# An expert loop in groups of four, with one token gather per group: a mixture-of-experts stage on one core

## The chip, the cores and the metric

One Trainium2 chip, one core of it. The metric is device time in microseconds (us) of one execution; less is better. All arithmetic is fp32 or fp32r (the form of fp32 that the kernel uses for products of a high and a low part).

## The reference, cut to what matters

A two-layer backbone over 256 latent tokens of width 1024 (with 256 context tokens in layer 0). Layer 0 has attention, a pooling mixer and a dense SwiGLU; layer 1 has a Fourier mixer and a top-2-of-8 expert SwiGLU. Only the last is touched:

```
logits = h @ router_w                      # (256, 8)
top_v, top_i = top_k(logits, 2); top_p = softmax(top_v)
gates  = sum(one_hot(top_i, 8) * top_p)    # (256, 8), two entries per token
y = 0
for e in range(8):
    y = y + gates[:, e:e+1] * ((silu(h @ w1[e]) * (h @ w3[e])) @ w2[e])   # widths 1024 -> 3584 -> 1024
```

h is 256 tokens x 1024, the weights of one expert are 42 MB (42 pieces of 1 MB), and they are all read from HBM once. The final RMSNorm follows.

## The kernel before, in words

**Routing.** After the Fourier mixer, TensorE computes the logits, turns them to token rows, turns h to token rows (h_tok, four banks copied by ScalarE, line 793) and, while VectorE ranks the tokens of each expert, runs a few matmuls on constants to fill the time (keep_warm). VectorE writes a table of ranks (line 1172), then the first choice of slots (picks(0), line 1200), then the gate values and the number of turns that the loops make (gates(), line 1176), in that order in its program.

**One turn** handles one expert and 96 of its tokens (CAP = 96). Two rounds would be made if an expert had more than 96 tokens; the trace shows eight turns, so one round. In a turn:

- gather (line 1625, TensorE): for every block of 128 rows of h, matmuls of h_tok with a 0/1 matrix pick (tokens x slots) put the 96 chosen tokens into banks 5 and 6. These are fp32 matmuls with 32 stationary columns each, four of them side by side in the array: 64 matmuls with 96 moving columns, which the trace records as 128. ScalarE (line 800) and VectorE (line 1211) copy the two banks to x_e, the x of this expert.
- up (line 1649) for four phases of the 3584 hidden units: w1 and w3 against x_e, 32 slots as the stationary operand, in banks 0 to 2. Line 1661 is its matmul.
- ScalarE takes silu (line 817), VectorE multiplies (line 1240) and turns blocks of 32 (line 1244).
- down (line 1666) for four phases, in banks 3 and 4. Line 1674 is its matmul.
- y of an expert is taken in the next turn (lines 807 and 1218), and TensorE spreads it back to its tokens with fp32r matmuls (combine, line 1636, matmul at 1641), which VectorE adds to x (line 1226).
- spreads (line 1681, matmuls at 1685 and 1689) makes the turned matrices for that.

**The order of the work** is written out by hand in each engine's program; semaphores join them. TensorE's turn i (expert, line 1692) is up and down of phases 0 to 3 with the rest of the previous expert between them; near its end it gathers for turn i + 1 (line 1723), and the last down of the turn covers the copies of that gather. Turn 0 is written out once in front (line 1728), and turns 1 to 7 are the body of a loop whose number of turns is read from memory (line 1732); ScalarE and VectorE have the same form (lines 836 and 1269). Ninth and last is a gather for a turn that is never made.

**The weights** are sent by SyncE's queue (line 500) into a ring of 16 slots of 1 MB, step by step: 12 steps a turn, and the pieces of a step are sent when TensorE has finished the step four before. This part has its own loop and isn't changed.

Of the kernel before, what the change touches and what calls it, by code (L numbers as in the profile page):

```python
# [15 lines left out]
P = 128  # L16
# [21 lines left out]
QUAD = 32  # L38
TRIPLES = CAP // QUAD
MAX_ROUNDS = -(-T // CAP)  # L40
TABLE = EXPERTS * (MAX_ROUNDS + 1)

# [134 lines left out]
def build(nc, vec_d, con_d, rope_d, x_d, ctx_d, ada_d, mixa_d, mixb_d, attn_d, mixout_d, ffn_d,  # L177
          dft_d, fnet_d, router_d, moe_d, out_d):
    ctx = ExitStack()
    with ctx:  # L180
# [10 lines left out]


        split = nc.alloc_sbuf_tensor_at("split", [P, 7 * PIECE], F32R, offset=ring_at + 4 * RING)
        xT = sb("xT", KD * T)
# [61 lines left out]
        ada_sum = view(work, 0, 2, 512)  # L256
        h_tok = view(work, 0, 2, D)
        x_e = view(work, 2048, KD, CAP)
        pick = view(work, 2816, 2, 2, P)
        rank_at = view(work, 3328, 2, TABLE)  # L260
# [18 lines left out]
        y_parts = [view(split, 4 * PIECE + n * D, D) for n in range(2)]  # L279
        spread = view(split, 4 * PIECE + 2 * D, 2, T)  # L280

        def plain(ap):
# [44 lines left out]
            sem("gap_ready"), sem("odds_ready"), sem("mask_ready"), sem("rank_ready"), sem("loops_ready"))  # L327
        pick_ready, gathered, x_first, x_second = sem("pick_ready"), sem("gathered"), sem("x_first"), sem("x_second")
        e_used, e_gate, e_hidden, e_turned = sem("e_used"), sem("e_gate"), sem("e_hidden"), sem("e_turned")
        y_high, y_low = ([sem(f"{name}{n}") for n in range(2)] for name in ("y_high", "y_low"))  # L330
# [277 lines left out]
        def _(act):  # L608
# [182 lines left out]
            for f in range(4):  # L791
                act.wait_ge(tok_ready, f + 1)
                nc.scalar.activation(h_tok[:, f // 2, (f % 2) * 512:(f % 2) * 512 + 512], bank[f][:, :], ACT.Copy).then_inc(tok_taken, 1)
# [24 lines left out]

            def expert(i):
                first = isinstance(i, int)  # L820
# [9 lines left out]
                take_gathered(i + 1)  # L830

            take_gathered(0)
            expert(0)
            act.wait_ge(loops_ready, 1)
            turns = act.value_load(loops[0:1, 0:1], min_val=EXPERTS, max_val=EXPERTS * MAX_ROUNDS)
            with nc.Fori(1, turns, engines=bass.OrderedEngineSet([act.engine]), hint_back_edge=True) as i:
                expert(i)
            take_y(turns, 0)

# [6 lines left out]
        def _(dve):  # L846
# [329 lines left out]
            def gates():  # L1176
# [15 lines left out]
                link(nc.vector.tensor_reduce(cols(210, 1), more, AX_X, ALU.add))  # L1192
                link(nc.vector.tensor_scalar(cols(211, 1), cols(210, 1), float(EXPERTS), float(EXPERTS), ALU.mult, ALU.add))
                link(nc.vector.tensor_scalar(cols(212, 1), cols(210, 1), 1.0, None, ALU.add))
# [12 lines left out]

            def take_gathered(i):

                dve.wait_ge(gathered, i + 1)  # L1210
                nc.vector.tensor_copy(x_e[:, 4:8, :], bank[6][:, 0:4 * CAP].rearrange("p (a b) -> p a b", a=4)).then_inc(x_second, 1)

# [32 lines left out]

            def expert(i):
                first = isinstance(i, int)
# [12 lines left out]
                hidden(i, 2)  # L1260
                hidden(i, 3)
                take_gathered(i + 1)

            picks(0)
            gates()
            take_gathered(0)
            expert(0)
            turns = dve.value_load(loops[0:1, 0:1], min_val=EXPERTS, max_val=EXPERTS * MAX_ROUNDS)
            with nc.Fori(1, turns, engines=bass.OrderedEngineSet([dve.engine]), hint_back_edge=True) as i:
                expert(i)  # L1270
            take_y(turns)
# [12 lines left out]
        def _(pe):  # L1284
# [363 lines left out]

            def up(i, phase, half, first):

# [5 lines left out]
                for k in range(4):  # L1656
                    for g in range(TRIPLES):
                        if half == 0 and k == 0 and not (first and phase == 0):
                            pe.wait_ge(e_hidden, PHASES * TRIPLES * i + TRIPLES * (phase - 1) + g + 1)
                        for c in range(4):  # L1660
                            last = mm(bank[g][c * QUAD:(c + 1) * QUAD, 0:count * P],  # L1661
                                      x_e[:, 4 * half + k, g * QUAD:(g + 1) * QUAD], source[:, :, k, :, c, :],
                                      start=(half == 0 and k == 0), stop=(half == 1 and k == 3), skip_group_check=True)
# [17 lines left out]
            def spreads(i):  # L1681

                for n in range(2):
# [7 lines left out]

            def expert(i):
                first = isinstance(i, int)
                pe.wait_ge(x_first, i + 1)
                pe.wait_ge(x_second, i + 1)
                up(i, 0, 0, first)
                up(i, 0, 1, first)
                if not first:
                    down(3, PHASES * TRIPLES * i, i, STEP_LAST)
                up(i, 1, 0, first)  # L1700
                if not first:
                    pe.wait_ge(spread_taken, i)
                    for pair in range(3):
                        combine(i, pair)
                up(i, 1, 1, first)
                if not first:
# [7 lines left out]
                spreads(i)  # L1714
                up(i, 2, 0, first)
                up(i, 2, 1, first)
                down(1, PHASES * TRIPLES * i + 6, i, STEP_OF["down", 1])
                up(i, 3, 0, first)
                up(i, 3, 1, first)
# [11 lines left out]
            turns = pe.value_load(loops[0:1, 0:1], min_val=EXPERTS, max_val=EXPERTS * MAX_ROUNDS)  # L1731
            with nc.Fori(1, turns, engines=bass.OrderedEngineSet([pe.engine]), hint_back_edge=True) as i:
                expert(i)
            down(3, PHASES * TRIPLES * turns, turns, 0)
            pe.wait_ge(x_first, turns + 1)
            pe.wait_ge(x_second, turns + 1)
            for pair in range(3):
# [72 lines left out]
```

## Time and profile before

| what | value |
|---|---|
| time, median of 3 runs | 1423.32 us (1421.16 to 1425.7) |
| the profiled execution | 1426.97 us |
| its span (first to last instruction) | 1425.2 us |
| mean granted TensorE clock | 0.991 of full |
| TensorE busy | 96% of the span |
| VectorE, ScalarE, GpSimd busy | 29%, 17%, 2% |
| HBM read | 454.76 MB, 320 GB/s over the span |
| expert turns, from the first up to the last down | 472.08 to 1409.74 us |

The page gives busy shares and the chain that ended last; the chain can also be asked for in order of time, and there each piece has its start, its length and what it was. A piece called issue is time in which the engine waited for nothing that the profile shows. L1661 is line 1661 of the kernel before.

### The profile page before, as it was taken

How to read it: one execution, taken by the hardware profiler on the slowest of the kernel's cores; microseconds unless marked ns; L12 is line 12 of the kernel's file. 1: busy time of each engine (PE TensorE's matmuls, PEld its weight loads, DVE VectorE, ACT ScalarE, POOL GpSimd, SP SyncE). 2: the span in 40 equal slices, each digit the busy share in tenths (PEclk: the TensorE clock that was granted, in tenths of full speed). 3: DMA queues.
4: the chain of work that ended last, by engine and by line, in shares of the span. 5: the costliest groups of instructions: out<-in, count | busy, mean ns of one | idle time of the engine just before them, and what ended most of it. 6: DMA issues, size and time to landing. Idle time of an engine off the chain costs nothing.

```text
span 1425.2 us, 30939 instructions
## 1 busy us (share of the span) xinstructions
PE 1364.1 (96%) x13838; PEld 737.1 (52%) x13838; DVE 412.2 (29%) x778; ACT 243.4 (17%) x410; POOL 21.7 (2%) x36
## 2 busy tenths in 40 slices
PE   5899899999999999999999999999999999999997
PEld 3755799999968434433433433423343353343334
DVE  2555579888434200010011001101001101110102
ACT  2444543333434100000000000000000000000002
POOL 2300000000000000000000000000000000000000
PEclk9899999999999999999999999999999999999999
DMA  9666259996616597997997999899799799889960
GB/s 382 258 237 237 94 222 354 353 372 259 226 41 275 219 364 305 418 418 299 396 414 295 415 389 374 337 383 422 288 417 418 295 414 410 358 351 410 422 277 31
DMA packets 58783, 457.83 MB, mean 321 GB/s; under 512 B 6656, under 2 KB 6784, under 8 KB 7584
## 3 DMA queue, kind: packets, MB, share of 16 engines
q1 hardware_dynamic: 58656, 455.84, 79.6%
q8 instruction: 116, 1.90, 0.5%
q14 instruction: 11, 0.09, 0.0%
HBM read 454.76 MB, written 1.05 MB: 320 GB/s over the span
## 4 chain that ended last, share of the span: by engine, by line
PE 94%; DVE 2%; issue 2%; DMA 1%; ACT 1%; SPq 0%; DVEq 0%; PEldq 0%; ACTq 0%
PE bank L1661 41%; PE bank L1674 20%; PE bank L1552 9%; PE bank L1542 4%; PE bank L1369 3%; PE bank L1632 2%; PE bank L1300 1%; PE bank L1406 1%; PE bank L1641 1%; PE bank L1473 1%; PE bank L1341 1%; PE bank L1576 1%; PE bank L1480 1%; PE bank L1588 1%; PE bank L1329 1%
## 5 line engine op out<-in xcount | busy, mean ns | idle before, releaser
L1661 PE MATMUL bank<-ring,work 128*32 128x512 f32 (+1 forms) x6144 | 588.6, 542 | 13.6 <-issue 11.9
L1661 PEld LDWEIGHTS bank<-ring,work 128*32 128x32 f32 x6144 | 208.4, 110 | 382.0 <-issue 348.3
L1674 PE MATMUL bank<-ring,moe 128*32 128x512 f32 x2688 | 294.9, 592 | 0.0
L1240 DVE TENSOR_TENSOR moe<-moe,bank 128x256 f32<-128x256 f32 (+1 forms) x96 | 31.5, 383 | 648.7 <-ACT moe L817 648.7
L1674 PEld LDWEIGHTS bank<-ring,moe 128*32 128x32 f32 x2688 | 99.1, 110 | 180.7 <-issue 179.2
L817 ACT ACTIVATE moe<-bank 128x256 f32<-128x256 f32 (+1 forms) x96 | 27.4, 358 | 737.0 <-PE bank L1661 737.0
L1552 PE MATMUL bank<-split 128*128 128x256 f32 x1056 | 131.2, 284 | 0.7 <-PE bank L1329 0.6
L1552 PEld LDWEIGHTS bank<-split 128*128 128x128 f32 x1056 | 128.0, 192 | 2.1 <-ACT split L748 1.3
L913 DVE TENSOR_TENSOR split<-ring,split 128x2048 fp32r<-128x2048 f32 x33 | 75.6, 2291 | 31.3 <-ACT split L754 24.3
L754 ACT ACTIVATE split<-ring 128x2048 fp32r<-128x2048 f32 x32 | 61.3, 1914 | 114.7 <-PE bank L1552 86.0
L928 DVE SCALAR_TENSOR_TENSOR work<-ring,condp,work 128x512 f32<-128x512 f32 x84 | 63.2, 752 | 3.7 <-DVE split L913 0.9
L1542 PE MATMUL bank<-split 128*128 128x256 f32 x480 | 59.5, 283 | 0.3 <-PE bank L1329 0.3
L1542 PEld LDWEIGHTS bank<-split 128*128 128x128 f32 x480 | 58.2, 192 | 0.4 <-issue 0.4
L1369 PE MATMUL bank<-split 128*128 128x256 f32 x384 | 47.0, 284 | 3.6 <-DVE split L1069 1.8
L1369 PEld LDWEIGHTS bank<-split 128*128 128x128 f32 x384 | 46.3, 192 | 4.1 <-DVE split L1069 2.2
L1226 DVE SCALAR_TENSOR_TENSOR xT<-bank,ada,xT 128x256 f32<-128x256 f32 x64 | 26.3, 472 | 62.2 <-PE bank L1641 62.2
L1406 PE MATMUL bank<-split 128*128 128x256 f32 (+1 forms) x192 | 31.5, 329 | 4.5 <-ACT split L624 4.0
L862 DVE TENSOR_TENSOR split<-ring,split 128x1024 fp32r<-128x1024 f32 (+1 forms) x24 | 28.5, 1207 | 15.9 <-ACT split L624 15.5
L1406 PEld LDWEIGHTS bank<-split 128*128 128x128 f32 x192 | 28.0, 205 | 7.8 <-ACT split L624 4.4
L1244 DVE STREAM_TRANSPOSE moe<-moe 128x256 f32<-128x256 f32 (+1 forms) x96 | 31.7, 381 | 0.0
L1204 DVE TENSOR_SCALAR work<-con,work 128x128 f32<-128x128 f32 x36 | 7.9, 282 | 75.1 <-PE bank L1689 75.1
L1300 PE MATMUL bank<-ring,condp 128*32 128x128 f32 x768 | 25.1, 286 | 4.5 <-DMA ring<-in_ada 4.0
(195 smaller groups left out, 730.4 us busy)
## 6 DMA issues: line engine op xcount, KB each, us to landing
ring<-in_moe SPq DMA_DIRECT2D x336, 1024.0 KB, 10.6
ring<-in_ffn SPq DMA_DIRECT2D x16, 2048.0 KB, 8.4
ring<-in_ada SPq DMA_DIRECT2D x12, 2048.0 KB, 8.8
ring<-in_ada SPq DMA_DIRECT2D x24, 1024.0 KB, 7.0
ring<-in_mixout SPq DMA_DIRECT2D x2, 2048.0 KB, 9.4
ring<-in_fnet SPq DMA_DIRECT2D x2, 2048.0 KB, 9.4
ring<-in_mixa SPq DMA_DIRECT2D x1, 2048.0 KB, 11.6
ring<-in_mixb SPq DMA_DIRECT2D x1, 1664.0 KB, 13.3
```

The source lines that it names most:

```text
L754: nc.scalar.activation(high_d[:, q % SPLITS_DENSE, :], piece_view(q), ACT.Copy).then_inc(high_ready, 1)
L913: nc.vector.tensor_tensor(low_d[:, q % SPLITS_DENSE, :], piece_view(q), plain(high_d[:, q % SPLITS_DENSE, :]), ALU.subtract).then_inc(low_ ...
L928: ins = nc.vector.scalar_tensor_tensor(out=total, in0=half_view(h)[:, k, :], scalar=weight, in1=total, op0=ALU.mult, op1=ALU.add)
L1240: nc.vector.tensor_tensor(gate_e[:, g, 0:n], gate_e[:, g, 0:n], bank[g][:, n:2 * n], ALU.mult).then_inc(e_hidden, 1)
L1244: nc.vector.transpose(hiddenT[phase % 2][:, g, 0:n], gate_e[:, g, 0:n]).then_inc(e_turned, 1)
L1300: last = mm(bank[RUNS[run][2]][32 * j:32 * j + 32, u * P:(u + 1) * P], cond[:, k, :], w[:, k, j * P:(j + 1) * P], start=(k == 0), stop=(k ...
L1369: last = mm(bank[banks[c // 2]][:, (c % 2) * T:(c % 2) * T + T], parts[left][:, k, j * P:(j + 1) * P], source[right][:, k0 + k, :], start= ...
L1406: last = mm(out, parts[left][:, k, lo:hi], h_in[right][:, k0 + k, 0:n], start=((left, right) == PRODUCTS[0] and k0 + k == 0 and opens), st ...
L1542: last = mm(bank[FFN_BANKS[k // 2]][:, (k % 2) * T:(k % 2) * T + T], w[:, j, k * P:(k + 1) * P], hidden_parts[g % 2][:, right, j, :], star ...
L1552: last = mm(bank[kind == "w3"][:, j * T:(j + 1) * T], w[:, k, j * P:(j + 1) * P], h_parts[:, right, k, :], start=(n == 0 and j == 0 and k ...
L1661: last = mm(bank[g][c * QUAD:(c + 1) * QUAD, 0:count * P], x_e[:, 4 * half + k, g * QUAD:(g + 1) * QUAD], source[:, :, k, :, c, :], start= ...
L1674: last = mm(bank[3 + n][c * QUAD:(c + 1) * QUAD, :], hiddenT[phase % 2][:, g, blk * QUAD:(blk + 1) * QUAD], source[:, j, n * 512:(n + 1) * ...
```

## The change

Turns are made in groups of four. In each engine's program the four turns of the first group are written out in front of the loop, and the loop's body holds the four turns of another group; for eight turns the body is run once. gather is made once per group, for 4 x 96 = 384 slots: 128 stationary columns of h_tok, 384 moving columns of a new matrix pick_group, both fp32r, with h_tok in a high and a low part (the low part is made by VectorE from the banks), three banks in turn, copied block by block by ScalarE (even blocks) and VectorE (odd blocks) to x_group. In the first group it stands ahead of turn 0, in the loop at the head of the body; its first up starts when four blocks are copied. pick (the matrix of spreads and combine) is kept, moved to another place in memory, and its wait moves to spreads. In VectorE's program the choice of 384 slots and the four low parts stand ahead of picks(0), and gates() and the copies of the first gather stay behind it. The filling matmuls move ahead of the wait for h_tok.

```
+GROUP = 4
+        x_group = view(work, 0, KD, GROUP * CAP)
+        pick = view(tail, 0, 2, 2, P)
+        pick_group = view(split, 4 * PIECE + 2 * D + 2 * T, 2, GROUP * CAP)
+        h_tok = [view(split, 2 * PIECE + n * 2 * D, 2, D) for n in range(2)]
 ScalarE
-            def take_gathered(i):
-                act.wait_ge(gathered, i + 1)
-                nc.scalar.activation(x_e[:, 0:4, :], bank[5][:, 0:4 * CAP].rearrange("p (a b) -> p a b", a=4),
-                                     ACT.Copy).then_inc(x_first, 1)
+            def take_gathered(group):
+                for k in range(0, KD, 2):
+                    act.wait_ge(gathered, KD * group + (k + 1))
+                    nc.scalar.activation(x_group[:, k, :], bank[5 + k % 3][:, 0:GROUP * CAP], ACT.Copy).then_inc(x_first, 1)
...
             take_gathered(0)
-            expert(0)
+            for j in range(GROUP):
+                expert(j, j == 0)
...
-            with nc.Fori(1, turns, ...) as i:
-                expert(i)
+            with nc.Fori(1, groups, ...) as group:
+                take_gathered(group)
+                for j in range(GROUP):
+                    expert(GROUP * group + j, False)
 VectorE
+            def group_picks(group):
+                for j in range(GROUP):
+                    for t in range(2):
+                        ins = nc.vector.tensor_scalar(pick_group[:, t, j * CAP:(j + 1) * CAP], C("slot_of")[:, P:P + CAP],
+                                                      rank_at[:, t, bass.ds(GROUP * group + j, 1)], None, ALU.is_equal)
+                ins.then_inc(group_picked, 1)
+            def token_lows():
+                for f in (0, 2, 1, 3):
+                    dve.wait_ge(tok_taken, f + 1)
+                    half = slice((f % 2) * 512, (f % 2) * 512 + 512)
+                    nc.vector.tensor_tensor(h_tok[1][:, f // 2, half], bank[f][:, :], plain(h_tok[0][:, f // 2, half]),
+                                            ALU.subtract).then_inc(tok_low, 1)
+            def take_gathered(group):
+                for k in range(1, KD, 2):
+                    dve.wait_ge(gathered, KD * group + (k + 1))
+                    nc.vector.tensor_copy(x_group[:, k, :], bank[5 + k % 3][:, 0:GROUP * CAP]).then_inc(x_second, 1)
...
+            dve.sem_inc(part_added[3], 1)
+            group_picks(0)
+            token_lows()
             picks(0)
             gates()
             take_gathered(0)
-            expert(0)
+            for j in range(GROUP):
+                expert(j, j == 0)
...
+            group_picks(1)
+            with nc.Fori(1, groups, ...) as group:
+                take_gathered(group)
+                for j in range(GROUP):
+                    expert(GROUP * group + j, False)
+                group_picks(group + 1)
 TensorE
-            def gather(i):
-                pe.wait_ge(pick_ready, i + 1)
+            def gather(group):
+                pe.wait_ge(group_picked, group + 1)
                 for k in range(KD):
-                    for t in range(2):
-                        for c in range(4):
-                            at = k * P + c * QUAD
-                            last = mm(bank[5 + k // 4][c * QUAD:(c + 1) * QUAD, (k % 4) * CAP:(k % 4 + 1) * CAP],
-                                      h_tok[:, t, at:at + QUAD], pick[:, 1, t, 0:CAP], start=(t == 0), stop=(t == 1))
-                last.then_inc(gathered, 1)
+                    if k >= 3:
+                        taken = x_first if k % 2 else x_second
+                        pe.wait_ge(taken, KD // 2 * group + ((k - 3) // 2 + 1))
+                    for n in range(2):
+                        if isinstance(group, int) and n == 1 and k % 4 == 0:
+                            pe.wait_ge(tok_low, k // 2 + 2)
+                        for t in range(2):
+                            last = mm(bank[5 + k % 3][:, 0:GROUP * CAP], h_tok[n][:, t, k * P:(k + 1) * P], pick_group[:, t, :],
+                                      start=(n == 0 and t == 0), stop=(n == 1 and t == 1))
+                    last.then_inc(gathered, 1)
...
+            def expert(i, j, first, group):
+                if j == 0:
+                    pe.wait_ge(x_first, KD // 2 * group + 2)
+                    pe.wait_ge(x_second, KD // 2 * group + 2)
+                up(i, j, 0, 0, first)
+                if j == 0:
+                    pe.wait_ge(x_first, KD // 2 * (group + 1))
+                    pe.wait_ge(x_second, KD // 2 * (group + 1))
+                up(i, j, 0, 1, first)
...
-                if not first:
-                    pe.wait_ge(part_added[3], i)
-                pe.wait_ge(spread_taken, i + 1)
-                gather(i + 1)
                 down(2, PHASES * TRIPLES * i + 9, i, STEP_OF["down", 2])
...
+            keep_warm(2, 7)
             pe.wait_ge(tok_taken, 4)
-            keep_warm(2, 7)
             gather(0)
-            expert(0)
+            for j in range(GROUP):
+                expert(j, j, j == 0, 0)
...
-            with nc.Fori(1, turns, ...) as i:
-                expert(i)
+            with nc.Fori(1, groups, ...) as group:
+                pe.wait_ge(part_added[3], GROUP * group)
+                pe.wait_ge(spread_taken, GROUP * group)
+                gather(group)
+                for j in range(GROUP):
+                    expert(GROUP * group + j, j, False, group)
```

## Rows read from the trace of the kernel before

**Rows 1.** The page: its span, and the chain that ended last by line

```profile
span 1425.2 us, 30939 instructions
...
PE bank L1661 41%; PE bank L1674 20%; PE bank L1552 9%; PE bank L1542 4%; PE bank L1369 3%; PE bank L1632 2%; PE bank L1300 1%; PE bank L1406 1%; PE bank L1641 1%; PE bank L1473 1%; PE bank L1341 1%; PE bank L1576 1%; PE bank L1480 1%; PE bank L1588 1%; PE bank L1329 1%
```

**Rows 2.** The chain in order of time, turn 5: start us, us, what

```profile
1053.46 1.57 issue
...
1157.32 2.71 PE bank L1632 x126
...
1170.41 1.84 issue
```

**Rows 3.** Waits of the whole span: total us, times, longest us

```profile
PE bank L1661 <- issue: 11.9, 6, 2.5
```

**Rows 4.** Stretches of the first 192 records of turns 2 and 3

```profile
700.07:720.87 20.80, 20.80 (x196) 6.63 (x200) 0.00 (x0) 0.00 (x0) 0.00 (x0) 1.00 0.92 377
...
817.38:839.88 22.50, 22.50 (x196) 6.97 (x200) 0.00 (x0) 0.00 (x0) 0.00 (x0) 0.92 0.93 381
```

The columns of rows 4 are the stretch, its length, busy us (records) of PE, PEld, DVE, ACT and POOL, PEclk, DMA share and GB/s.

**Rows 5.** The chain in order of time, from turn 0's gather to turn 2's

```profile
567.91 1.71 PE bank L1632 x81
569.62 0.37 issue
...
571.19 10.30 PE bank L1674 x95
581.49 20.60 PE bank L1661 x192
...
617.54 1.62 PE bank L1641 x12
...
683.58 1.64 PE bank L1632 x76
685.22 0.70 issue
...
687.27 10.30 PE bank L1674 x94
...
802.36 2.64 PE bank L1632 x128
```

**Rows 6.** The chain in order of time, first gather and first up

```profile
468.51 2.89 PE bank L1632 x128
...
472.08 20.84 PE bank L1661 x192
```

**Rows 7.** VectorE's instructions in order of time, picks(0) to its first copy

```profile
467.58 0.88 DVE L1204 TENSOR_SCALAR work<-con,work 128x128 f32<-128x128 f32 x4
468.37 0.17 DVE L1180 TENSOR_SCALAR small<-small 128x2 f32<-128x2 f32 x1
...
471.38 0.06 DVE L1198 MEMSET small<- 128x1 f32 x1
471.42 0.56 DVE L1211 COPY work<-bank 128x384 f32<-128x384 f32 x1
```

**Rows 8.** Groups of instructions by line and shape: busy us, mean ns, idle before

```profile
L1552 PE MATMUL bank<-split 128*128 128x256 f32 x1056 | 131.2, 284 | 0.7 <-PE bank L1329 0.6
...
L1632 PE MATMUL bank<-work 128*32 128x96 f32 x1152 | 26.4, 246 | 1.1 <-issue 1.1
...
L856 DVE TENSOR_TENSOR split<-bank,split 128x512 fp32r<-128x512 f32 x12 | 8.2, 691 | 16.0 <-ACT split L781 10.5 <-ACT split L778 5.5
```

**Rows 9.** TensorE in order of time, second half of the input projection

```profile
55.74 16.95 PE L1406 MATMUL bank<-split 128*128 128x256 f32 x96
```

**Rows 10.** DMA of turn 3, 815 to 934 us: rate in 40 slices, queues

```profile
GB/s 421 424 408 430 306 220 419 427 391 372 421 432 419 427 424 419 427 416 421 419 419 430 416 413 58 39 416 256 0 251 419 427 375 402 421 419 435 416 421 424
...
q1 hardware_dynamic: 6060, 44.13, 90.6%
q8 instruction: 11, 0.18, 0.6%
```

More of the change, by code:

```diff
@@ L190, in build @@
         sb("split_end", 5 * PIECE)
+        tail = nc.alloc_sbuf_tensor_at("tail", [P, 2816], F32, offset=ring_at + 4 * (RING + 11520))
         split = nc.alloc_sbuf_tensor_at("split", [P, 7 * PIECE], F32R, offset=ring_at + 4 * RING)
@@ L817, in gates, with expert @@
                     nc.scalar.activation(gate_e[:, g, 0:n], bank[g][:, 0:n], ACT.Silu).then_inc(e_gate, 1)
-            def expert(i):
-                first = isinstance(i, int)
+            def expert(i, first):
                 gates(i, 0, first)
@@ L829, in expert @@
                 gates(i, 3, first)
-                take_gathered(i + 1)
             take_gathered(0)
-            expert(0)
+            for j in range(GROUP):
+                expert(j, j == 0)
             act.wait_ge(loops_ready, 1)
-            turns = act.value_load(loops[0:1, 0:1], min_val=EXPERTS, max_val=EXPERTS * MAX_ROUNDS)
-            with nc.Fori(1, turns, engines=bass.OrderedEngineSet([act.engine]), hint_back_edge=True) as i:
-                expert(i)
-            take_y(turns, 0)
+            groups = act.value_load(loops[0:1, 0:1], min_val=EXPERTS // GROUP, max_val=EXPERTS // GROUP * MAX_ROUNDS)
+            with nc.Fori(1, groups, engines=bass.OrderedEngineSet([act.engine]), hint_back_edge=True) as group:
+                take_gathered(group)
+                for j in range(GROUP):
+                    expert(GROUP * group + j, False)
+            take_y(GROUP * groups, 0)
             nc.scalar.activation(small[:, 242:243], C("eps"), ACT.Sqrt)
@@ L1244, in hidden, with expert @@
                     nc.vector.transpose(hiddenT[phase % 2][:, g, 0:n], gate_e[:, g, 0:n]).then_inc(e_turned, 1)
-            def expert(i):
-                first = isinstance(i, int)
+            def expert(i, first):
                 hidden(i, 0)
@@ L1266, in _ @@
             take_gathered(0)
-            expert(0)
-            turns = dve.value_load(loops[0:1, 0:1], min_val=EXPERTS, max_val=EXPERTS * MAX_ROUNDS)
-            with nc.Fori(1, turns, engines=bass.OrderedEngineSet([dve.engine]), hint_back_edge=True) as i:
-                expert(i)
+            for j in range(GROUP):
+                expert(j, j == 0)
+            groups = dve.value_load(loops[0:1, 0:1], min_val=EXPERTS // GROUP, max_val=EXPERTS // GROUP * MAX_ROUNDS)
+            group_picks(1)
+            with nc.Fori(1, groups, engines=bass.OrderedEngineSet([dve.engine]), hint_back_edge=True) as group:
+                take_gathered(group)
+                for j in range(GROUP):
+                    expert(GROUP * group + j, False)
+                group_picks(group + 1)
+            turns = GROUP * groups
             take_y(turns)
@@ L1647, in landed_wait, with up @@
                 pe.wait_ge(piece_in[step % FOURS][at], 16 * loads_at(i, step, at))
-            def up(i, phase, half, first):
+            def up(i, j, phase, half, first):
                 step = STEP_OF["up", phase, half] + (first and phase == 0)
@@ L1661, in up @@
                             last = mm(bank[g][c * QUAD:(c + 1) * QUAD, 0:count * P],
-                                      x_e[:, 4 * half + k, g * QUAD:(g + 1) * QUAD], source[:, :, k, :, c, :],
+                                      x_group[:, 4 * half + k, j * CAP + g * QUAD:j * CAP + (g + 1) * QUAD], source[:, :, k, :, c, :],
                                       start=(half == 0 and k == 0), stop=(half == 1 and k == 3), skip_group_check=True)
@@ L1681, in spreads @@
             def spreads(i):
+                pe.wait_ge(pick_ready, i + 1)
                 for n in range(2):
@@ L1690, in spreads @@
                 last.then_inc(spread_turned, 1)
[L1692 to L1697, printed above, removed]
+            def expert(i, j, first, group):
[7 more added lines that the diff above has]
+                up(i, j, 0, 1, first)
                 if not first:
                     down(3, PHASES * TRIPLES * i, i, STEP_LAST)
-                up(i, 1, 0, first)
+                up(i, j, 1, 0, first)
                 if not first:
                     pe.wait_ge(spread_taken, i)
+                    pe.wait_ge(part_added[3], i)
                     for pair in range(3):
                         combine(i, pair)
-                up(i, 1, 1, first)
+                up(i, j, 1, 1, first)
                 if not first:
@@ L1714, in expert @@
                 spreads(i)
-                up(i, 2, 0, first)
-                up(i, 2, 1, first)
+                up(i, j, 2, 0, first)
+                up(i, j, 2, 1, first)
                 down(1, PHASES * TRIPLES * i + 6, i, STEP_OF["down", 1])
-                up(i, 3, 0, first)
-                up(i, 3, 1, first)
-                if not first:
-                    pe.wait_ge(part_added[3], i)
-                pe.wait_ge(spread_taken, i + 1)
-                gather(i + 1)
+                up(i, j, 3, 0, first)
+                up(i, j, 3, 1, first)
                 down(2, PHASES * TRIPLES * i + 9, i, STEP_OF["down", 2])
+            keep_warm(2, 7)
             pe.wait_ge(tok_taken, 4)
-            keep_warm(2, 7)
             gather(0)
-            expert(0)
+            for j in range(GROUP):
+                expert(j, j, j == 0, 0)
             pe.wait_ge(loops_ready, 1)
-            turns = pe.value_load(loops[0:1, 0:1], min_val=EXPERTS, max_val=EXPERTS * MAX_ROUNDS)
-            with nc.Fori(1, turns, engines=bass.OrderedEngineSet([pe.engine]), hint_back_edge=True) as i:
-                expert(i)
+            groups = pe.value_load(loops[0:1, 0:1], min_val=EXPERTS // GROUP, max_val=EXPERTS // GROUP * MAX_ROUNDS)
+            with nc.Fori(1, groups, engines=bass.OrderedEngineSet([pe.engine]), hint_back_edge=True) as group:
+                pe.wait_ge(part_added[3], GROUP * group)
[3 more added lines that the diff above has]
+                    expert(GROUP * group + j, j, False, group)
+            turns = GROUP * groups
             down(3, PHASES * TRIPLES * turns, turns, 0)
-            pe.wait_ge(x_first, turns + 1)
-            pe.wait_ge(x_second, turns + 1)
+            pe.wait_ge(part_added[3], turns)
+            pe.wait_ge(spread_taken, turns)
             for pair in range(3):
```

13 lines of the change are left out of this document (4 added, 9 removed).

## The prediction

> **What bounds the kernel now.** I read the page first: the chain that ended last lies on TensorE almost throughout, 61% of it in the matmuls of up and down (L1661 and L1674) [rows 1]. Those are not touched, so the question is what lies between them. The chain in order of time shows it. Turn 5 lasts from 1053.46 to 1170.41, 116.95 us, and in it stand one gather (L1632, 2.71 with its small remainders) and, before its first up, a piece of 1.57 called issue; everything else, 112.6 us, is up, down, combine and spreads back to back [rows 2]. TensorE is late for no other engine there. The waits say that such pieces came six times ahead of L1661, 11.9 us in all [rows 3], and in the chain they stand where turns 2 to 7 begin, never elsewhere in a turn. Turn 1, the first of the loop, begins at 581.49, which is 571.19 + 10.30: no gap, though the same code is entered there in sequence [rows 5]. Six gaps for six jumps back to the loop's head, and none where it is entered from above: I take the gap as the price of the jump.
>
> **The change, part by part.**
>
> Jumps back. Eight turns need six jumps now and none afterwards, since the body of four turns runs once. That takes away 11.9 us. [...] Two times 1.70 is 3.4 us. Together **-15.3**.
>
> Small gathers. Nine are made; the first is costed below with the start. Of the eight others the first two have a stall inside: 567.91 to 571.19 is 3.28, and 683.58 to 687.27 is 3.69 [rows 5]. The six others take 2.64 (four) or 2.75 (two) [rows 2, 5], 16.1. Together 23.0; the group row agrees, 26.4 busy less the first 2.9, plus 1.1 idle, less some 0.2 at each of eight ends that overlap the next matmul [rows 8]. **-23.0**.
>
> The large gather. 8 blocks x 2 parts x 2 halves of tokens = 32 matmuls with 384 moving columns. No row has that width in fp32r. With 256 columns one takes 131.2 / 1056 = 0.124 us [rows 8]. The 96 of the second half of the input projection are 48 of 256 and 48 of 512 columns and took 16.95 [rows 9]; less 48 x 0.124 that leaves 0.229 for 512. 384 lies in the middle: 0.177, so 5.7 us a gather. The ends are 0.124 and 0.229, that is 4.0 and 7.3. [...]
>
> In the second group, at the head of the loop's body, those 5.7 us stand on the path whole. Its waits cost nothing: each block is 0.71 us of matmul, a bank comes round after three blocks, and a copy of 128x384 takes 0.56 on VectorE [rows 7]; block 3 was copied long before the last block ends, so the first up follows at once, and the copies of blocks 4 to 7 hide under its 10.4 us. VectorE's choice of slots for it (about 1.4 us) hides under the last down of turn 3, 10.30. If that cover failed, the 1.4 would show. **+5.7**. Both ends of the gather change between 32 and 128 stationary columns. The nearest row is the combine, 12 fp32r matmuls of 256 columns between ups, 1.62 us or 0.135 each against 0.124: 0.13 for a pair of such changes, within my rounding, below nothing excluded [rows 5]. [...]
>
> The first gather. Now it starts at 468.51, and the first up at 472.08 [rows 6]. Afterwards VectorE is in the way. The rank table is ready at 467.58, where picks begins. Eight choices of 96 columns replace four of 128 as the first thing; four take until the next instruction's start 0.79, 0.197 each [rows 7], and a quarter fewer columns make that about 0.165 (ends: 0.165 and 0.197, so 1.3 or 1.6). TensorE may start at 469.0. The four low parts follow, 0.69 each [rows 8]: two done at 470.3, four at 471.7. TensorE does the high half of block 0, waits to 470.4, then blocks 0 to 3, until about 473.0. Block 4 needs block 1 out of its bank, and that copy is VectorE's, behind picks(0) (0.8) and the whole of gates(): 468.37 to 471.42, 3.05 us [rows 7]. So gates() ends at 471.7 + 0.8 + 3.05 = 475.5, the copy at 476.1, and TensorE stands idle for 3.1 us. Then blocks 4 to 7, 2.8 us; the first up at 479.0 instead of 472.1. **+6.9**, between 6 and 8.
>
> The clock there. [...] Between 0 and 3.4 us (none, or twice what rows 4 show); I take one such loss. **+1.7**.
>
> Costed at nothing: the writes of h_tok as fp32r, picks(i + 1), which hides under up as now, the extra wait in spreads for picks done a turn earlier, the wait of combine for a sum added a turn earlier, and the last choice of slots, under the final downs. The weights: a turn moves 44.13 MB, and the queue reaches 421 GB/s where it is busy, 105 us; the rate falls to nothing in the middle of a turn, because the ring is full [rows 10]. A turn of 112.6 us needs 392 GB/s. It stays below, but the cover shrinks from 12 us to 8 a turn.
>
> Sum: -15.3 - 23.0 + 5.7 + 6.9 + 1.7 = **-24.0 us**. The profiled execution took 1426.97 (span 1425.2 [rows 1] and 1.8 around it), so 1403.0. That execution lies 3.65 above the median of the runs, 1423.32; against the median the forecast is **1399.3 us**. A measurement of this kernel can tell about 0.3%, 4.3 us, from no change.
>
> **The rivals.**
>
> A: the gaps are not the jump's but come with a turn's first up (its waits, or its weights), and stay. Then 15.3 us are not won: 1414.6. For it: DMA is fully busy in these stretches. Against it: turn 1 has no gap [rows 5], and by the ring's rate step 0 has landed some 13 us before. 6%.
>
> B, slower than before: the supply of instructions. Turn 3 fetched 11 packets of code [rows 10], and the gathers of 567.91 and 683.58 have stalls of 0.37 and 0.70 in straight code, with the weights' traffic at full rate [rows 5]. If written-out turns stalled so at each of 11 packets, 88 times 0.37 is 33 us, and 1432 us comes out. It decides from 0.27 us a packet (24 / 88). Against it: turn 0 is straight code and has one such stall, and it is in the small gather, the densest stretch of instructions, which goes. 4%.
>
> C: the fp32r gather doesn't run at the rate of the other fp32r products, or its first run with VectorE is longer than counted (the clock down twice, gates() late), some 6 to 12 us more: 1405 to 1411. Small parts of this are in my range. 9%.
>
> D: no effect of unlooping beyond the gathers and no start stall, because VectorE's queue is less in the way than I think: 1391 to 1393. 3%.
>
> **The numbers.** My forecast has 78%, with its own range 1392 to 1407: 3.4 up and down for the large matmuls, 1.7 for the clock, 1 for the start and about 2 for what runs differ, not all at once. The range is taken to 1410 for most of C. Faster by over 0.3%: all but B and what the sum could have missed, 93%; within 0.3%: 3%; slower: 4%.
>
> **What would show it.** Right: the chain has no issue piece where turns 1 to 7 begin; turns of 112.6 us; the records of the new gather some 0.18 us apart; two stretches of idle TensorE in the first gather, about 1 and 3 us, the second until VectorE's copy of block 1; the first up near 479; the first up of turn 4 right behind its gather. Wrong: gaps of about 2 us at any turn's start (A), many stalls of 0.3 us within turns (B), a gather of over 7.3 us in the loop, or the first up later than 481 (C). A time above 1410 would mean that one of the first two terms is not what I took it for.

## The result, and the profile after

The changed kernel takes **1402.6 us** (median of 4 runs, 1402.07 to 1403.28) against 1423.65 of the kernel before (median of 4, 1421.16 to 1425.7): a ratio of 0.9853, 95% interval 0.9836 to 0.987, 21.05 us less. Its profiled execution took 1402.48, 24.5 less than the profiled one of before.

The page of the changed kernel, span and chain by line (L1697 is up, L1710 down, L1668 the gather):

```profile
span 1400.7 us, 28586 instructions
...
PE bank L1697 41%; PE bank L1710 21%; PE bank L1584 9%; PE bank L1574 4%; PE bank L1401 3%; PE bank L1332 2%; PE bank L1438 1%; PE bank L1677 1%; PE bank L1505 1%; PE bank L1373 1%; PE bank L1608 1%; PE bank L1512 1%; PE bank L1620 1%; PE bank L1668 1%; PE bank L1361 1%
```

What bounds the kernel is as in [rows 1]; only the pieces between have gone. The chain in order of time, from the end of turn 1 to the first up of turn 4:

```profile
689.47 10.30 PE bank L1710 x96
699.76 20.60 PE bank L1697 x192
...
801.85 10.30 PE bank L1710 x96
812.14 20.60 PE bank L1697 x192
...
914.23 10.30 PE bank L1710 x96
924.52 5.78 PE bank L1668 x32
930.30 20.74 PE bank L1697 x192
```

Where [rows 2] have a narrow gather ahead of the last down and an issue piece behind it, up of the next turn follows at once; a turn is 812.14 - 699.76 = 112.4 us. The large gather of the second group stands whole on the path with 5.78 us, 0.181 a matmul, and its first up follows without a wait.

The same view at the first gather, which answers to [rows 6, 7]:

```profile
468.62 1.53 DVE split L1219 x8
470.14 2.39 DVE split L1228 x4
472.53 0.78 DVE tail L1211 x4
...
476.01 0.17 DVE loops L1204
...
476.23 0.56 DVE work L1235
476.79 0.04 issue
476.83 4.47 PE bank L1668 x16
481.31 20.78 PE bank L1697 x192
```

From 468.62 to 476.79 the chain is VectorE's own program order: choice of slots, low parts, picks(0), the chain of gates(), and only then the copy that TensorE waits for. The last 16 matmuls then take 4.47 us, against 2.89 for 16 of the second group. The stretches of both, with the columns of [rows 4], say why: the first was done at a granted clock of 0.65 (0.50 from 476.80 to 479.80), the second at 1.00.

```profile
476.80:481.30 4.50, 4.47 (x20) 4.22 (x24) 1.00 (x2) 1.12 (x3) 0.00 (x0) 0.65 0.02 4
...
924.52:930.30 5.78, 5.78 (x37) 5.53 (x40) 1.68 (x3) 1.97 (x4) 0.00 (x0) 1.00 1.02 424
```

DMA of turn 3 (812 to 924 us), which answers to [rows 10]:

```profile
GB/s 424 421 421 421 413 424 421 424 418 415 421 418 424 418 415 424 421 418 421 418 421 421 421 415 421 252 348 380 3 85 430 424 421 342 424 424 424 421 427 413
...
q1 hardware_dynamic: 6027, 43.88, 95.2%
```

The rate still falls to almost nothing once a turn (3 GB/s in one slice), and TensorE has no wait for weights in the turns: they are not late, with less in hand.

**Where the 24.5 us of the two traces come from.** From the first up to the last down of the expert turns it was 937.7 us and is 903.8, 33.8 less. The six gaps are 11.9 of it, the two slow starts 3.4, the eight narrow gathers 23.0; the second large gather gives back 5.8; the remaining 1.3 are the six starts behind a gap, which took 20.81 where the clock stayed up, against 20.60 now for five of them and 20.74 behind the large gather. The first up begins at 481.31 instead of 472.08, 9.2 later, of which 0.9 was there before the gather: the matmuls that fill the time ahead of the ranks begin at 466.11 instead of 465.19 (in the front part TensorE waited 5.2 instead of 4.0 us for one piece of ada weights). The other 8.3 are the first gather's.

### The profile page after: what moved, and what is told of

Read it like the earlier page. It is cut to its first block, busy times and chain, and to the rows that moved or that the text cites. A ratio compares the mean times of both kernels' runs of the same rounds, so it can differ in the third digit from the quotient of the medians.

```text
span 1400.7 us, 28586 instructions
## 1 busy us (share of the span) xinstructions
PE 1347.4 (96%) x12750; PEld 704.5 (50%) x12750; DVE 418.3 (30%) x805; ACT 242.9 (17%) x409; POOL 21.7 (2%) x36
## 3 DMA queue, kind: packets, MB, share of 16 engines
q8 instruction: 102, 1.67, 0.5%
## 4 chain that ended last, share of the span: by engine, by line
PE 94%; DVE 3%; DMA 1%; ACT 1%; issue 1%; SPq 0%; DVEq 0%; PEldq 0%; ACTq 0%
PE bank L1697 41%; PE bank L1710 21%; PE bank L1584 9%; PE bank L1574 4%; PE bank L1401 3%; PE bank L1332 2%; PE bank L1438 1%; PE bank L1677 1%; PE bank L1505 1%; PE bank L1373 1%; PE bank L1608 1%; PE bank L1512 1%; PE bank L1620 1%; PE bank L1668 1%; PE bank L1361 1%
## 5 line engine op out<-in xcount | busy, mean ns | idle before, releaser
L1697 PE MATMUL bank<-ring,work 128*32 128x512 f32 (+1 forms) x6144 | 584.9, 539 | 1.1 <-DVE moe L1264 1.1
L1697 PEld LDWEIGHTS bank<-ring,work 128*32 128x32 f32 x6144 | 199.7, 110 | 373.2 <-issue 340.3
L1710 PE MATMUL bank<-ring,moe 128*32 128x512 f32 x2688 | 294.3, 593 | 0.0
L1710 PEld LDWEIGHTS bank<-ring,moe 128*32 128x32 f32 x2688 | 87.5, 110 | 193.5 <-issue 191.2
L1211 DVE TENSOR_SCALAR tail<-con,work 128x128 f32<-128x128 f32 x36 | 7.9, 283 | 74.7 <-PE bank L1726 74.7
```

The lines of the kernel that those rows point to most:

```text
L1697: last = mm(bank[g][c * QUAD:(c + 1) * QUAD, 0:count * P], x_group[:, 4 * half + k, j * CAP + g * QUAD:j * CAP + (g + 1) * QUAD], source[: ...
L1710: last = mm(bank[3 + n][c * QUAD:(c + 1) * QUAD, :], hiddenT[phase % 2][:, g, blk * QUAD:(blk + 1) * QUAD], source[:, j, n * 512:(n + 1) * ...
```

## The experiments

**1. Turns written out, nothing else.** Theory: the gap is the price of the jump. Rivals: it belongs to a turn's first up, or to the supply of instructions.

```
 (the kernel before, in all three programs)
-            expert(0)
+            for j in range(4):
+                expert(j, j == 0)
...
-            with nc.Fori(1, turns, ...) as i:
-                expert(i)
+            with nc.Fori(1, groups, ...) as group:
+                for j in range(4):
+                    expert(4 * group + j, False)
```

> The kernel before with nothing changed but the form of the loop: turns 0 to 3 written out, the body of the loop holds four turns, the small gather of every turn stays. Theory (the gap is the jump's price): no issue piece where turns 1 to 7 begin, turns of 115.0 to 115.4 us (112.4 to 112.6 and a gather of 2.6 to 2.8), time below the kernel before by 13.2 us (11.9 for six gaps and about 0.2 for the slower restart of each) plus 1.7 for every lower-clock stretch that an execution of the kernel before has: 13 to 17 us, about 1408. Rival A (the gap belongs to a turn's first up): gaps of 1.6 to 2.5 stay at 4 to 7 of the starts and the time stays within 3 us of 1423. Rival B (supply of instructions in straight code): gaps vanish from the starts but stalls of 0.3 to 0.7 come up inside turns, as in the gathers at 567 and 683 us of before.

Measured: 1414.34 us (1413.89 to 1417.36), ratio 0.9939 (0.9921 to 0.9958), 9.8 less than the 1424.13 of the runs beside it. No gap at any start, which is against rival A. The 13 to 17 us expected were missed. The chain, gathers ahead of turns 2 and 5:

```profile
684.02 1.88 PE bank L1639 x89
685.90 0.76 issue
686.65 0.95 PE bank L1639 x36
...
1031.34 1.97 PE bank L1639 x94
1033.31 0.27 issue
1033.58 0.93 PE bank L1639 x33
```

Seven of the eight gathers of turns 0 to 7 have such a stall or slow stretch, against two in the kernel before; the eight together take 25.6 us instead of 23.0. The expert turns are 13.8 us shorter than in the trace of before: 16.3 won at the starts (gaps, slow starts, slower restarts), 2.5 of it lost inside the gathers. The rest of what is missing against the medians is that this trace of before is one of the longer executions (experiment 5). So rival B holds in part, and only where 64 narrow matmuls are issued in 2.6 us.

**2. The first gather's copies ahead of gates().**

```
 (the changed kernel, VectorE)
             token_lows()
+            take_gathered(0)
             picks(0)
             gates()
-            take_gathered(0)
```

> The changed kernel with VectorE's four copies of the first gather moved ahead of picks(0) and gates(). Theory (TensorE's 2.7 us of idle time in the first gather are VectorE's queue, and the lower clock behind it is the idle time's): the idle piece goes, the first gather's second half takes 2.9 instead of 4.5 us, the first up starts 4.3 us earlier, and the time falls by 4 to 4.5 us to about 1398.3. Rival (gates() is needed early, and what waits for it becomes late): the first up starts earlier, but a later piece of turn 0 waits for VectorE, and the time falls by less than 2 us.

Measured: **1398.1 us** (1397.64 to 1399.61), ratio 0.9822 (0.98 to 0.9845), the fastest kernel here that computes the whole result. The chain:

```profile
471.83 5.47 PE bank L1668 x30
477.30 20.78 PE bank L1697 x192
```

30 matmuls in one piece, 0.182 each, and an up that starts 4.0 us earlier, though the matmuls ahead of the ranks come 0.45 later in this execution. The idle time and the slow stretch were both VectorE's queue, and no wait for gates() shows in turn 0.

**3. Filling the stall.**

```
 (the changed kernel, TensorE, in gather)
+                    if isinstance(group, int) and k == 4:
+                        keep_warm(5, 0)
                     if k >= 3:
```

> The changed kernel with five filling matmuls on constants (keep_warm, 128x256 fp32, 2.2 us or so) between blocks 3 and 4 of the first gather, in the time in which TensorE waits for VectorE. They add nothing to the result. Theory (the 4.5 us of the second half are a lower clock, brought by the idle time): the wait stays until about 476.8, the second half falls from 4.5 to 2.9 us at a granted clock of 1.00, the time falls by 1.6 us to 1401.0. Rival (the second half is slow for another reason, such as copies and banks): it stays at 4.5 and the time stays at 1402.6.

Measured: 1400.76 us (1400.55 to 1401.8), 1.8 less than the changed kernel's 1402.6. The copy that TensorE waits for ends at 476.24. That is 0.55 before 476.79, and as much earlier as the choice of slots begins in this execution (468.08 against 468.62), so the filling hasn't moved it. The second half takes 3.05 instead of 4.47, at a granted clock of 1.00:

```profile
475.68 0.56 DVE work L1235
476.25 0.04 issue
476.29 3.05 PE bank L1670 x16
```

So 1.4 us of the second half were the clock, which stayed at 1.00 with matmuls in the idle time, and neither banks nor copies.

**4. Groups of two.** GROUP = 2 in the changed kernel, so two jumps.

> The changed kernel with groups of two turns (GROUP = 2): the body of the loop is run three times, so two jumps, and four gathers of 192 slots. Theory: a gap of 1.6 to 2.5 us ahead of the gather where turns 4 and 6 begin and none elsewhere; gathers of 3.2 to 3.6 us (0.10 to 0.11 a matmul); together 4 to 5 for the jumps, plus 1.5 to 3 for the gathers, less about 2.5 in the first gather (four choices of slots less, narrower matmuls in the slow stretch): 1405 to 1409. Rival A (the gap belongs to the turn's start): gaps at all starts or none.

Measured: 1407.53 us (1406.97 to 1408.39), ratio 0.9886 (0.9863 to 0.9908), within the range, but for another reason. The chain at the first of the two jumps:

```profile
907.87 10.36 PE bank L1697 x192
918.23 10.30 PE bank L1710 x96
928.53 3.75 PE bank L1668 x32
```

918.23 + 10.30 is 928.53: **no gap at a jump**, and none at the other. The time is that of the gathers: three of 3.75 stand in the loop where one of 5.78 stood (a matmul of half the columns takes 0.117, not half of 0.181), 5.5 us more. These two jumps cost nothing, so a jump as such isn't the price; my theory had to be replaced.

**5. The kernel before, once more**, to see what varies in it.

> The kernel before, unchanged, profiled a second time. The forecast's size missed by some 3 us against the medians, while it fits the two profiled executions. Theory (what a jump costs varies from execution to execution): the gaps ahead of turns 2 to 7 again sum to 9 to 14 us but not one by one the same, the number of starts at the lower clock is another (0 to 4), and the two profiled executions differ by these pieces and by less than 0.5 us elsewhere in the expert turns; ten executions spread over more than 5 us. Rival (the executions vary elsewhere, in the first 460 us): the expert turns agree within 1 us.

Measured: 1425.21 us, 12 runs from 1419.86 to 1426.76. The profiled one took 1421.72, 5.3 less than the first. Its waits, against [rows 3]:

```profile
PE bank L1661 <- issue: 9.9, 6, 2.7
```

It has no start at the lower clock. Its expert turns last from 472.20 to 1404.51, 932.3 us, 5.35 less than in the first trace: 2.0 in the gaps and 3.4 in two slow starts, and nothing is left over. These two executions of the kernel differ by what they lose at the jumps; that the other runs do too isn't shown, as only these two have a trace. The changed kernel's four lie within 1.2 us.

**6 to 8. The hint and the place of the loop's head.** Experiment 6 leaves out the hint that hint_back_edge puts at the head of a loop; 7 and 8 set the instruction slot of its block at which TensorE's loop begins.

```
 (the kernel before, TensorE's loop; 6: in all three programs)
 6: -   hint_back_edge=True
    +   hint_back_edge=False
 7: +   head_slot={pe.engine: 0}
 8: +   head_slot={pe.engine: 239}
```

> [...] The groups of two showed no gap at their two jumps, so a jump as such isn't the price. [...] Theory 2 (the hint does nothing in this loop): no change within 2 us.

> The kernel before with TensorE's loop placed so that its first instruction is the first of a block of 256 in the program. Theory 1 (where the head stands in its block decides: a body entered near a block's end needs the next block at once): the gaps ahead of turns 2 to 7 vanish or fall under 0.3 us, and the time falls by 12 to 16 us to 1408 to 1412. Theory 2 (what follows the jump decides: an up with its register waits, against a gather in the groups of two): the gaps stay at 1.5 to 2.5 and the time stays at 1424.

> The same with the loop's first instruction as number 239 of a block of 256, so that 17 instructions of the body are left in it. Theory 1: gaps of 2 us or more at all six jumps, 1422 to 1430. Theory 2: the same gaps as in the kernel before and with the head at 0.

Measured: without the hint 1447.3 us (ratio 1.0149, 1.0125 to 1.0172); head at 0 1440.47 (1.0105, 1.0082 to 1.0129); head at 239 1444.07 (1.0121, 1.0094 to 1.0147). Without the hint, the start of turn 2 in the chain:

```profile
697.51 4.60 issue
702.11 22.91 PE bank L1661 x192
```

All six gaps are 4.0 to 4.6 there, 26.2 in sum, and all six starts behind them are slow (22.4 to 23.8). With the hint, in the first trace of before, they are 1.57 to 2.50, and two starts of the six are slow (22.50): 2.4 us less a jump on average, and most of the clock loss gone, so Theory 2 is wrong. What the hint does in the chip isn't shown by this; experiment 12 has the packets of code. The span is 25.0 us longer than in that trace: the gaps are 14.3 longer in sum, and the starts lose 11 more, which I had not counted.

Placing the head at 0 didn't remove the gaps; they grew to 2.6 to 3.2 us, so Theory 1 as I put it is wrong. The entry to the placed loop also has a gap, where [rows 5] have none; the traces have one instruction more than that of before (30940 against 30939), which I take for a jump over the space left free; the runs don't show what it is. Head at 0, then head at 239, the entry of turn 1:

```profile
582.91 1.58 issue
584.50 20.81 PE bank L1661 x192
```

```profile
582.01 0.84 PE bank L1661 x5
582.86 0.96 issue
583.81 20.36 PE bank L1661 x186
```

With the head 17 instructions short of its block's end the gap comes behind the first few matmuls of the body, not ahead of them. A jump does bring the gap here, and its place and size depend on where the code lies; but neither placement made it vanish. Not all of the 16 to 20 us lie at the jumps: the narrow gathers stall more as well, the eight taking 25.3 us (7) and 28.0 (8) instead of 23.0.

**9 to 11. What lies ahead of the jump.** The groups of two had no gap: by the length of their body (L), or because the narrow gather shortly before the jump was gone (D)?

```
 9:  the changed kernel        -GROUP = 4   +GROUP = 1
10:  experiment 1              -GROUP = 4   +GROUP = 2
11:  the kernel before, TensorE's gather
-                for k in range(KD):
+                for k in range(KD) if isinstance(i, int) and i == 0 else (0, 4):
```

> The changed kernel with groups of one turn (GROUP = 1): one turn in the loop's body, six jumps as before the change, and a gather of 96 slots (32 fp32r matmuls with full-width stationary operands) at the head of every turn, in place of the 64 narrow fp32 ones near its end. Theory D (the gap needs a dense stretch of instructions shortly before the jump: the narrow gather issues four times as many matmuls in half the time, uses up what was fetched ahead, and the jump's target comes late): no gap above 0.3 us at the six jumps, gathers of 2.9 to 3.8 us, 1416 to 1422. Theory L (the length of the body or its place among the blocks decides, a body of two turns being free of gaps by its length): gaps of 1.4 to 3 us at the six jumps, 1428 to 1438.

> The kernel before with its narrow gather in every turn and nothing changed but groups of two turns, two jumps. Theory D: gaps of 1.4 to 3 us at both jumps (ahead of turns 4 and 6) and none elsewhere, 1417 to 1421. Theory L: no gap at either, as in the groups of two with the large gather, about 1414.

> The kernel before, one turn in the body, with a quarter of the gather of turns 1 to 8 (blocks 0 and 4 of the eight; the other blocks of x are then left out, and the experts are computed with what lies in the banks). A gather of 0.66 us instead of 2.64 takes 16 us away by itself. Theory D: with 32 records instead of 128 the gaps at the six jumps fall under 0.5 us as well, another 8 to 15 us: 1393 to 1400. Theory L: the gaps stay within 1 us of what they were in sum, 1405 to 1409.

Measured: 1423.77 us (ratio 0.999, 0.998 to 1.0), 1416.88 (0.9949, 0.9929 to 0.9969) and 1393.61 (0.9776, 0.9759 to 0.9792); the kernel before took 1426.23 beside them. Experiment 11 leaves six of the eight blocks of x out, so it is there for its time alone. That time was given by D and not by L; experiment 10's lies 0.1 under D's range. The chain of 9, of 10 and of 11 at one jump each:

```profile
690.27 10.30 PE bank L1710 x96
700.57 3.70 PE bank L1668 x32
```

```profile
917.95 10.30 PE bank L1681 x94
928.25 1.86 issue
930.11 20.81 PE bank L1668 x192
```

```profile
682.18 0.66 PE bank L1632 x32
682.84 10.30 PE bank L1674 x96
693.14 20.60 PE bank L1661 x192
```

With one turn in the body and six jumps, but no narrow gather, there is no gap (9); with two turns and the narrow gather both jumps have one, 1.86 and 1.81 (10); with a quarter of the gather none of six has (11). The body's length doesn't decide. Experiment 9 missed its time although its gaps are as D says: its gathers take 3.70 each, near the top of what was expected, and two starts were slow (21.90 and 22.43). The second of these, turn 4's at 936.74, had no gap ahead: TensorE was busy throughout from 920.00 at a granted clock of 1.00, and the start's is 0.92. So the slow starts behind gaps need not be the gaps' doing in every case.

**12. The narrow gather in three parts.** Is it the density of instructions in that gather?

```
 (the kernel before, TensorE; gather(i, lo, hi) makes blocks lo to hi - 1)
-                gather(i + 1)
-                down(2, PHASES * TRIPLES * i + 9, i, STEP_OF["down", 2])
+                down(2, PHASES * TRIPLES * i + 9, i, STEP_OF["down", 2], ((0, 3), (3, 6), (6, 8)))
```

> The kernel before, one turn in the body and six jumps, with the whole narrow gather, but made in three parts (blocks 0 to 2, 3 to 5, 6 and 7) ahead of the first, second and third quarter of the last down of the turn, 2.6 us of down behind each. Nothing is left out. Theory D (the density of instructions shortly before the jump, not the presence of a jump or of this gather): no stall inside a gather, the gaps at the six jumps fall from 10 to 12 us in sum to under 4, and no start at the lower clock; 1411 to 1417. Rival (what counts is how many instructions lie in the last 13 us before the jump, however spread): the gaps stay at 9 to 12 us in sum, and the time at 1424.

Measured: 1424.84 us (12 runs, 1421.05 to 1431.5), ratio 1.0005 (0.9988 to 1.0022): the rival. The chain at the start of turn 2:

```profile
685.19 0.99 PE bank L1633 x48
686.18 2.57 PE bank L1678 x24
688.75 0.99 PE bank L1633 x48
689.74 2.57 PE bank L1678 x24
692.32 0.66 PE bank L1633 x32
692.98 5.15 PE bank L1678 x48
698.13 1.44 issue
```

The stalls inside the gathers are gone, but the gaps are not: 11.2 us in six, against 11.9 in [rows 3], and two starts at 22.50. The rival's 13 us, taken as they stand, don't separate the kernels either. In them TensorE works off 176 to 228 matmul records ahead of the gaps of the kernel before, and 172 in experiment 11 and 149 in experiments 4 and 9, which have none, and one gap of experiment 8 has only 143. Over the last 15 us the two kinds are apart: 235 to 264 records ahead of each gap that I counted, 208 and 185 without.

The traces also show the code arriving. It comes in packets of 16 KB on the queue that the page lists as q8 instruction (102 packets, 1.67 MB, in the changed kernel), and the time of each can be read to some 0.05 us:

| one jump of each kernel | jump | last packet ahead of it, next one | first matmul behind it |
|---|---|---|---|
| the kernel before | 697.57 | 696.74, 702.65 | 700.07 |
| experiment 6, no hint | 697.51 | 696.24, 698.96 | 702.11 |
| experiment 12 | 698.13 | 696.21, 701.52 | 699.57 |
| experiment 9 | 700.57 | 693.12, 701.74 | 700.57, no gap |
| experiment 11 | 693.14 | 685.94, 694.25 | 693.14, no gap |
| experiment 4 | 928.53 | 920.73, 929.67 | 928.53, no gap |

In both traces of the kernel before and in experiments 6, 7, 10 and 12 there are 33 gaps of 1.4 to 4.6 us, and every one ends 3.1 to 3.4 us after a packet: with the hint one that moved in the last 1.9 us ahead of the gap or at its start, without it one that moved 0.8 to 1.5 us after its start. The gaps of experiment 8, behind the first matmuls of the body, end 2.4 to 2.6 after one. In experiments 4, 9 and 11 the last packet lies 6.3 to 8.2 us ahead of each of the 14 jumps. I read the gap as the wait for that packet of code, and what the narrow gather changes is that one more packet moves just ahead of the jump. Why fewer records shift it is open, and so is what part the place of the body's end in its block has. A late packet alone isn't enough: where the kernel before enters its loop from above, at 581.49, one moved 1.7 us ahead and there is no gap.

## Why the prediction was right, and its size a little off

**Jumps back, -15.3.** In the two profiled executions this is what went, 11.9 and 3.4, and 1.3 more in the restarts, which I had left out. The 3.4 in the forecast are the starts of turns 3 and 4, 22.50 us each where others take 20.80, at a granted clock of 0.92 instead of 1.00 [rows 4]; in both it stood at 0.50 for some 3 us. I put that down to the length of the gap, and the runs don't show this: gaps of 2.07 and 2.22 stood ahead of these two, but the gap of 2.50 and those of 1.84, 1.65 and 1.57 left the clock at 1.00, and experiment 9 has a slow start without a gap. The reading "I take the gap as the price of the jump" was the step that failed as an explanation: experiments 4 and 9 jump without a gap. The gap takes a jump and a packet of code that moves just ahead of it or later (experiment 12), and with a wide gather in place of the narrow one six jumps have none (experiment 9). Writing out the turns alone, with the narrow gather kept, is worth 9.8 us against the median; the narrow gathers get 2.5 us slower by it (experiment 1). Each part of the change by itself removes the gaps, so their effects can't be added.

**Small gathers, -23.0, and the large one, +5.7.** Eight went and one of 5.78 came. A matmul of 384 columns took 0.181, against 0.177 from the rows. At the change from the gather's 128 stationary columns to the 32 of up no more than 0.14 us shows (the first up of turn 4 takes 20.74 where the other starts take 20.60).

**The start, +6.9, and its clock, +1.7.** 8.3 us were measured for 8.6. VectorE's eight choices, four low parts, picks(0) and gates() came in the order and nearly the lengths worked out (1.53, 2.39, 0.78, and 2.9 for gates()), the idle piece was 2.7 instead of 3.1 us, and the slow stretch 1.6. Experiment 2 takes both away and experiment 3 the slow stretch alone.

**The sum against the median.** -24.0 was forecast, and the traces show -24.5. The failing step is the one that put the sum against the median: "That execution lies 3.65 above the median of the runs" was treated as an offset that stays, so 1399.3. But what made that execution long was part of what the change removes: two starts at the lower clock and the longer gaps (experiment 5, another execution, loses 5.35 less, all of it there). The changed kernel's execution has no such excess (1402.48 against a median of 1402.6). The term of the jumps was taken from one of the longer executions; at the median it was about 3 us smaller, an estimate from the 3.3 by which that execution lies above 1423.65. 1402.6 lies in the forecast's own range, 1392 to 1407.

**The rivals.** A fell with experiment 1. B was right about the kind of stall and wrong about its place: in straight code it comes up in the narrow gather (0.24 to 0.76 us in experiment 1) and in no up or down of that trace, and the changed kernel has none. C and D didn't occur. D's time, 1391 to 1393, leaves out the start's stall alone; had the gaps stayed as well, as its first words say, it would have been 15.3 more. The weights came in time, as costed; the cover that shrank was not used up.

## What to carry to other kernels

Before writing out a loop to save its jumps, look at what TensorE does in the last fifteen microseconds ahead of the jump, and at when the packets of code move: the gap here came with the jump and 235 or more matmul records before it, and fewer, wider matmuls removed it as well. When the profiled execution is off the median, ask which of the pieces you are about to remove vary between executions, and take their price at the median. And when work moves ahead of a first use, read the other engines' program order: 4.5 us of this change's cost was one call standing behind another on VectorE, and moving it made the fastest whole kernel of the study, 1398.1 us.

## What the runs showed of the hardware that was not expected

- Jumps back of this loop, in its several forms, cost 0 (experiments 4, 9, 11), 1.4 to 2.7 us (the kernel before), 2.5 to 3.2 (other places of the loop's head) or 4.0 to 4.6 (without the hint). Without the hint a packet of code moves 0.8 to 1.5 us after the gap's start, and the gap ends 3.1 to 3.2 us after it. With the hint, and 208 or 185 matmul records in the last 15 us, there was no gap.
- Packets of code move in straight code too (11 in turn 3 of the kernel before [rows 10]), and up and down ran on almost without a stall: none in the turns of the changed kernel and of experiment 1, one of 0.41 us in experiment 8, at 1422.51, in the down behind the loop. In the narrow gather, 64 matmuls in 2.6 us with DMA at 415 to 426 GB/s, there are stalls of 0.24 to 0.76 us in straight code (experiment 1), and up to 1.50 (experiment 8, at 807.75). Five of them (two in the kernel before, two in experiment 1, one in 8) end 2.3 to 2.5 us after a packet of code.
- Placing a loop's head at a chosen slot of its block cost 16 to 20 us in all. In the expert turns of the two traces 6.4 (head at 0) and 5.7 us (at 239) are gaps, with the one at entry, and 2.2 and 4.9 the narrow gathers.
- The granted clock fell, to 0.50 for some 3 us, behind gaps of 2.07 and 2.22 us and not behind one of 2.50 (the kernel before), and once with no idle time ahead (experiment 9, 0.92 from 936.74 on).
- An fp32r matmul with 128 stationary columns took 0.116 us for 96 moving columns (experiment 9), 0.117 for 192 (experiment 4), 0.124 for 256 [rows 8] and 0.181 for 384; below 256 columns there is little to be won by narrowing it.
